# Three low-part subtractions and a gate product take other places in VectorE's order

## The reference, cut to what matters

```
h = x @ w_in
q, f, i, g = split(h)
q = silu(q);  fg = lb + (1 - lb) * sigmoid(f);  k = 1 - fg
S_t = diag(fg_t) S_{t-1} + k_t v_t^T ;  o_t = S_t^T q_t        # per head, v = i
o = rms_norm(o, g_norm) * silu(g)
return o @ w_o
```

## Time and profile before

| | |
|---|---|
| median of 3 runs | 948.1 us (947.6 to 949.48) |
| profiled execution, its own time | 948.63 us |
| span of its trace | 946.8 us |
| TensorE busy | 920.9 us, 97% |
| VectorE busy | 587.4 us, 62% |
| ScalarE busy | 458.0 us, 48% |
| recurrence, first level to the end of its outputs | about 362 to 415 us from the span's start |

### The profile page before, as it was taken

The page is one execution under the profiler, slowest core; times in us unless marked ns, Lnnn a source line. Parts: engine busy times, 40 slices in busy tenths (PEclk is TensorE's granted clock), DMA queues, the critical chain, the costliest instruction groups (busy, mean ns, idle before and its releaser), DMA issues.

```text
span 946.8 us, 13782 instructions
## 1 busy us (share of the span) xinstructions
PE 920.9 (97%) x5667; PEld 759.6 (80%) x5667; DVE 587.4 (62%) x916; ACT 458.0 (48%) x609; POOL 155.9 (16%) x128
## 2 busy tenths in 40 slices
PE   7989999999999999899999999999999999999996
PEld 6857788888887997688888888878777788888885
DVE  5874773644648579878636455494323567777775
ACT  5766352534333443543435243445656465564653
POOL 3265300000005400013000000040455201010011
PEclk9999999999999999999999999999999999999999
DMA  8981465555646654235755555548433465555531
GB/s 300 203 162 51 171 223 179 179 191 199 187 160 205 213 166 149 91 133 192 231 178 189 198 191 178 177 159 308 135 133 91 154 214 184 180 178 178 181 130 45
DMA packets 104382, 164.91 MB, mean 174 GB/s; under 512 B 4027, under 2 KB 74730, under 8 KB 104320
## 3 DMA queue, kind: packets, MB, share of 16 engines
q1 hardware_dynamic: 101056, 152.61, 48.6%
q0 software_dynamic: 3264, 11.42, 5.6%
HBM read 159.83 MB, written 4.19 MB: 173 GB/s over the span
## 4 chain that ended last, share of the span: by engine, by line
PE 85%; DVE 7%; ACT 4%; issue 1%; DMA 1%; POOL 1%; SPq 0%; DVEq 0%; POOLq 0%; ACTq 0%
PE PG L1800 12%; PE PG L1802 12%; PE PG L1801 12%; PE PA L1800 12%; PE PA L1802 12%; PE PA L1801 11%; DVE wlo L600 1%; ACT whi L591 1%; PE PG L1936 1%; PE TB L2388 1%; DVE work L1527 1%; PE TB L2051 1%; PE PA L2205 1%; PE PA L2204 1%; PE PA L2203 1%
## 5 line engine op out<-in xcount | busy, mean ns | idle before, releaser
L600 DVE TENSOR_TENSOR wlo<-raw,whi 128x2048 fp32r<-128x2048 f32 (+1 forms) x124 | 289.1, 2348 | 62.9 <-ACT whi L591 62.8
L591 ACT ACTIVATE whi<-raw 128x2048 fp32r<-128x2048 f32 (+1 forms) x142 | 268.6, 1908 | 47.7 <-PE PA L1802 18.5
L1800 PE MATMUL PG<-whi,xlo 128*128 128x512 f32 x548 | 218.3, 398 | 0.7 <-DVE wlo L1331 0.6
L1802 PE MATMUL PG<-whi,xhi 128*128 128x512 f32 x548 | 214.4, 391 | 0.0
L1801 PE MATMUL PG<-wlo,xhi 128*128 128x512 f32 x548 | 214.0, 391 | 0.0
L1800 PEld LDWEIGHTS PG<-whi,xlo 128*128 128x128 f32 x548 | 103.2, 188 | 22.1 <-DVE wlo L1331 1.3
L1802 PEld LDWEIGHTS PG<-whi,xhi 128*128 128x128 f32 x548 | 103.2, 188 | 22.0
L1801 PEld LDWEIGHTS PG<-wlo,xhi 128*128 128x128 f32 x548 | 103.3, 188 | 19.9
L1800 PE MATMUL PA<-whi,xlo 128*128 128x512 f32 (+1 forms) x292 | 117.3, 402 | 1.8 <-DVE xlo L1107 1.3
L1802 PE MATMUL PA<-whi,xhi 128*128 128x512 f32 (+1 forms) x292 | 112.6, 385 | 0.0
L1801 PE MATMUL PA<-wlo,xhi 128*128 128x512 f32 (+1 forms) x292 | 112.2, 384 | 0.0
(11 more groups left out here) (289 smaller groups left out, 1169.4 us busy)
## 6 DMA issues: line engine op xcount, KB each, us to landing
raw<-in_ffn_w_gate SPq DMA_DIRECT2D x44, 512.0 KB, 3.9
raw<-in_ffn_w_up SPq DMA_DIRECT2D x44, 512.0 KB, 4.9
raw<-in_ffn_w_down SPq DMA_DIRECT2D x22, 1024.0 KB, 4.8
raw<-in_w_up SPq DMA_DIRECT2D x44, 512.0 KB, 4.8
raw<-in_hgrn_w_in SPq DMA_DIRECT2D x16, 1024.0 KB, 5.3
raw<-in_w_qkv SPq DMA_DIRECT2D x12, 1024.0 KB, 5.1
raw<-in_w_down SPq DMA_DIRECT2D x11, 1024.0 KB, 4.8
raw<-in_att_w_o SPq DMA_DIRECT2D x4, 1024.0 KB, 5.4
```

Of the source, the lines that this page charges most:

```text
L591: nc.scalar.activation(whi[:, g, 0:n_], raw[:, s, 0:n_], ACT.Copy).then_inc(S("w_hi"), 1)
L600: nc.vector.tensor_tensor(wlo[:, s, 0:n_], raw[:, s, 0:n_], whi[:, g, 0:n_].bitcast(F32), ALU.subtract).then_inc(S("w_lo"), 1)
L1800: mm(dst, xl[:, k, rows], whi[:, g, cols], start=first, stop=False)
L1802: return mm(dst, xh[:, k, rows], whi[:, g, cols], start=False, stop=last_)
```

## The change

Nothing is added or removed. The low parts of U_H+15, U_H+16 and U_H+17 and the gate's product go to other places in VectorE's list.

```
             take(1)
-            lo(U_H + 15)
             decayed(2)
             take(2)
-            lo(U_H + 16)
             decayed(3)
             take(3)
             decayed(4)
-            vec.wait_ge(S("g_sig"), 1)
-            link(ve_.tensor_tensor(flat(sg), flat(sg), flat(fT), ALU.mult))
+            lo(U_H + 15)
             decayed(5)
...
                 ve_.tensor_copy(flat(aT[:, 2, 4 * b:4 * b + 4, :]), TB[:, b, :]).then_inc(S("aT2"), 1)
-            lo(U_H + 17)
+            vec.wait_ge(S("g_sig"), 1)
+            link(ve_.tensor_tensor(flat(sg), flat(sg), flat(fT), ALU.mult))
...
             gained_lo(0)
+            lo(U_HO)
+            lo(U_HO + 1)
             lo(U_HO + 2)
```

## The result

The changed kernel takes 951.18 us (median of 8 runs, 949.56 to 952.67) against 947.97 for the kernel before: a ratio of 1.0031, 95% interval 1.002 to 1.0042. It is 3.2 us slower, where 0.9 slower was the forecast; The range was 947.4 to 951.1; the time lies 0.1 us past its upper end, and as a ratio to the kernel before it lies at that end (1.0031 against 951.1 / 948.1 = 1.0032), on the side of the two slower rivals. A second measurement gave 950.81 (12 runs) against 947.87, ratio 1.0026 (1.0016 to 1.0035). The profiled execution took 950.64, only 2.0 more than that of the kernel before, and its span is 948.7. So there are two differences to explain: the 2.0 us between the profiles, and the rest up to 3.2.

What follows compares the result with a forecast made beforehand. TensorE, busy 97% of the span, was taken as the bound, waiting for VectorE around the levels. A 2.8 us later tail less 1.9 us won in the levels gave 0.9 slower, 949.0 us; range 947.4 to 951.1.

Steps and rivals of the forecast that it cites:

- the two slower rivals: Longer TensorE wait at level 5, 2.3 to 2.6 us slower, chance 0.22; clock drop in the tail, 2.6 slower, 0.12.
- D: Output projection: its third unit, U_HO+2, starts 2.8 us later because three low parts stand where one did.
- The three gaps: TensorE's tail: waits of 0.35 us before U_HO, 1.1 before U_HO+1, and up to 426.8 before U_HO+2.
- the rival of the free tail: Behind the output projection: something gives the tail's delay back, so 1.9 to 3.1 us faster; chance 0.06.
- The levels up to level 5: Level 4 starts at 384.6 instead of 386.74; take(4) moves 0.46; most of 2.3 us won becomes a wait for ScalarE.
- The stall: TensorE idle 1.68 us inside level 5, no releaser shown; if it goes, the next tile starts 1.3 us earlier.
- g: The levels, to the end of level 6: they end earlier by 0.2 to 3.1 us, taken as 1.9.
- the third line: Level 6 ends at 396.8 to 397.6, with a clock drop over the work as before: 0.5 to 1.3 us earlier.
- The lull: Level 5: TensorE's longer wait for take(4) keeps the clock low afterwards, 2.3 to 2.6 us slower; chance 0.22.
- D - g: Whole kernel: tail delay less the levels' gain, 2.8 - 1.9 = 0.9 us slower.
- The clock in the tail: Rival: waits between 420.7 and 426.8 bring a half-clock stretch costing 1.7 us, 2.6 slower in all; chance 0.12.

Runs made afterwards that it cites:

- tail alone: The changed kernel with VectorE's passes in the levels as before, an unread subtraction standing in for the moved passes: 950.68 us, ratio 1.0029.
- the fourth experiment: The changed kernel with U_HO's and U_HO+1's low parts in VectorE's idle places, and ScalarE's gate sigmoid moved from before take(4) to behind take(5): 945.13 us, ratio 0.9973.
- the first experiment: The changed kernel with U_HO's low part moved behind decayed(5) and U_HO+1's behind gated(1), where VectorE stood idle: 947.74 us, ratio 0.9994.
- the kernel with the filled lull: The changed kernel with ten spare matmuls in TensorE's wait at level 5, their results unread: 949.77 us, ratio 1.0017.
- the one with a low part in the tail: The changed kernel with U_HO's low part moved behind decayed(5) and U_HO+1's left behind gained_lo(0): 947.34 us, ratio 0.9999.
- shifted kernel: The kernel before with four of eleven warming matmuls replaced by 68 small ones, 128 more TensorE instructions near the start: 965.66 us, ratio 1.0194.

## Why the prediction was right or wrong, point by point

- **D, 2.8.** Right: 2.83 or 2.84 in three profiles of the changed kernel, 2.8 as a median of its own (tail alone), 0.62 with one low part less (0.6 to 1.0 expected). The three gaps came at their places with their releasers, and nothing behind took them back, so the rival of the free tail falls.
- **The levels up to level 5.** Right: level 4 at 384.66 (384.6 said), the next tile at 391.8 (391.6), `take(4)` moved by 0.41 (0.46). The 2.1 us won at level 4 turned into a wait for ScalarE, and the fourth experiment shows that it was the bound: 1.7 us at like clock, 2.6 in the median, came back when its sigmoid went behind it. The stall fell away inside that wait.
- **g, 1.9.** Wrong, and the one mis-sized term of the sum: 1.1 to 1.2 was measured, and 1.15 by the kernel without the tail. The lines for g set ends of the changed kernel with a mild low stretch, or none, against an end of the kernel before that had a full one in it (398.08). That counted the luck of the clock as a gain of the change. Set like against like, from the prediction's own rows, the terms were 0.46 of the moved tile and 0.85 of the lost stall, 1.3 in all. The profiled execution fell on the third line (396.96; 396.8 to 397.6 said), which the prediction held less likely than the value it took. With g = 1.1 to 1.2 the forecast would have been 1.6 to 1.7 slower, and two profiles at held clock differ by 1.68.
- **The lull.** That it is longer and brings the clock down oftener was told as a rival with 0.22, at 2.3 to 2.6 us. Its mechanism is in the result: the median sits 1.4 to 1.5 above D - g, the kernel with the filled lull takes most of it back, and 16 of 21 runs against 20 of 90 lie in the upper group. The rival's form differs: not the stall's return and two low stretches, but one, in most runs. The lower clock is common where the lull is (mean 0.996 or less in 16 of 21, eight of 11 and five of 11 runs of the changed kernel, the first experiment and the one with a low part in the tail) against 37 of 82 in the kernel before, and rare where the lull is filled or the sigmoid late (none of 11 and one of 11). The Trainium skill, "TensorE: Matmul & The Clock Gate", section "Part 1: The HAM clock gate", says that the window runs free of the kernel; profiles of the changed kernel with (950.64) and without (949.66) a low stretch behind the same lull agree with that.
- **The clock in the tail.** It was 1.00 over the tail's gaps in every profile that has them. This rival did not show.
- **The stall.** The prediction left open whether it was a fetch. It is bound to a grid of 256 instructions (shifted kernel). The Trainium skill, "Runtime: NRT & Kernel Launch", section "Instruction fetch mechanics", says that the blocks are of 256 instructions, and the grid agrees. It also says that crossing from one to the next is mostly hidden: 44 of 45 are in the kernel before, and the one that is not, among small matmuls, took 1.68 us there and 3.02 with the late sigmoid.
- **The chances.** 0.60 lay on no measurable difference and 0.34 on slower, and slower it was: 3.2 us, with an interval of 1.9 to 4.0 against the 1.9 that the prediction took as its bound. With like set against like, the forecast itself would have stood at 1.7, just under the bound of 1.9, and every low stretch more in the changed kernel would have carried it over.

That the result came out at the range's end and not outside it is luck in part: the sum lacked 0.7 to 0.8 us in g and the 1.5 of the clock, and the range was wide enough only because the slower rivals had been counted into it.

What stays open: the record has the mean clock of each timed run and not where in the run it was low, so that the low stretch of the upper group lies behind the lull is shown by the filled lull and by single profiles, not run by run. The execution that took 950.85 had its low stretch elsewhere, so not all of the upper group is the lull's. Why the fetch comes late (its packet starts 0.65 us before the stall in the kernel before, when the transfer of a weight unit has just ended) wasn't tried.

## What to carry to other kernels

Before work is moved from a full stretch of an engine to a later one, look for that engine's idle stretches and the wait that ends next in both places. Here one low part more in the tail cost 0.6 us, the second 2.2, and the same two in idle places cost nothing. When a pass moves behind a long stage, ask what produces its input: that the gate's product came later paid only once the sigmoid, 1.9 us on the path, had gone behind the levels too. And compare ends of stages at the same granted clock; a low stretch in the one profile there is of the kernel before is not a cost that the change will remove.

## What the runs showed of the hardware that was not expected

- Two executions of one kernel with the same gaps differ by 1.0 us, 950.64 and 949.66; the first has a half-clock stretch behind the lull of TensorE and the second has none, which is 1.5 us between the start of level 3 and the end of level 6.
- The same fetch stall is 0.55, 1.68 or 3.02 us long in single profiles of kernels whose TensorE instructions are the same, and it does not show where TensorE waits there anyway.
- With four of the 11 warming matmuls at the start replaced by 68 small ones (128 instructions more) the clock was low for 13.7 us there, and the kernel lost 18 us in the median. Whether the missing matmuls or the added ones did it wasn't told apart.
